# Other joints between the stages of a one-core transformer stack on Trainium2

## The reference

```python
def rms_norm(x, w):
    y = x * lax.rsqrt(jnp.mean(x * x, axis=-1, keepdims=True) + EPS)
    return y * w
# a layer of the first block; the second block has the same shape
mix = mixer(rms_norm(h, norm_pre), ...)            # products, heads, output product
h = h + rms_norm(mix, norm_post)
u = relu(rms_norm(h, mlp_norm_pre) @ w_up)
h = h + rms_norm((u * u) @ w_down, mlp_norm_post)
# second block, last steps
f = (silu(g @ w_gate) * (g @ w_up)) @ w_down       # g = rms_norm(x, ffn_pre_norm)
x = x + rms_norm(f, ffn_post_norm)
x = x + sigmoid(x @ w_ple_gate) * rms_norm(p @ w_ple_proj, ple_norm)
```

## Time and profile before

| what | before |
|---|---|
| median of 3 runs | 1039.75 us (1038.03 to 1039.81) |
| the profiled execution's own time | 1038.76 us |
| its span, first to last instruction | 1037.0 us |
| mean granted TensorE clock | 0.993 |
| PE / PEld / DVE / ACT / POOL busy | 97% / 88% / 71% / 53% / 9% |

### The profile page before, as it was taken

How to read it: one execution, slowest core, us unless ns; L and a number is a source line. 1 busy time by engine, 2 the same in 40 slices (tenths; PEclk the granted TensorE clock), 3 DMA queues, 4 the chain that set the end, 5 groups by cost and what they waited for, 6 DMA issues and landing times.

```text
span 1037.0 us, 18064 instructions
## 1 busy us (share of the span) xinstructions
PE 1002.9 (97%) x6615; PEld 910.1 (88%) x6615; DVE 737.2 (71%) x1095; ACT 550.7 (53%) x824; POOL 89.9 (9%) x94
## 2 busy tenths in 40 slices
PE   6999999999999999998999999998998999999998
PEld 5999988888888989997788888998997888888887
DVE  5787676878764498765977744478778887776466
ACT  5743255655454465655655534445556555555445
POOL 5214101000100200002000100100001000000010
PEclk9999999999999999999999999999999999999999
DMA  8543444466666745434366565625525366665641
GB/s 261 151 124 119 123 122 143 146 198 183 190 185 193 234 132 173 135 122 141 119 208 186 178 193 187 182 74 163 164 82 164 117 183 184 186 196 172 195 145 62
DMA packets 164702, 166.27 MB, mean 160 GB/s; under 512 B 6784, under 2 KB 162832, under 8 KB 164640
## 3 DMA queue, kind: packets, MB, share of 16 engines
q1 hardware_dynamic: 162752, 163.47, 52.3%
q0 software_dynamic: 1056, 1.16, 0.5%
q10 hardware_dynamic: 832, 0.79, 0.3%
HBM read 163.79 MB, written 1.08 MB: 159 GB/s over the span
## 4 chain that ended last, share of the span: by engine, by line
PE 85%; DVE 9%; ACT 3%; issue 2%; DMA 1%; POOL 1%; SPq 0%; DVEq 0%; ACTq 0%; POOLq 0%
PE ps L597 30%; PE ps L596 16%; PE ps L580 4%; PE ps L581 4%; PE ps L582 4%; PE ps L593 3%; PE ps L823 3%; DVE w_lo L1820 2%; PE ps L574 2%; PE ps L576 2%; PE ps L575 2%; PE ps L594 2%; PE ps L587 1%; PE ps L588 1%; PE ps L589 1%
## 5 line engine op out<-in xcount | busy, mean ns | idle before, releaser
L1820 DVE TENSOR_TENSOR w_lo<-w_raw,w_hi 128x1024 fp32r<-128x1024 f32 (+3 forms) x318 | 379.2, 1198 | 156.3 <-ACT w_hi L1302 152.2
L1302 ACT ACTIVATE w_hi<-w_raw 128x1024 fp32r<-128x1024 f32 x302 | 317.4, 1054 | 205.5 <-PE ps L597 91.6
L597 PE MATMUL ps<-xs,w_hi 128*128 128x512 f32 x840 | 296.8, 396 | 0.0
L596 PE MATMUL ps<-xs,w_lo 128*128 128x256 f32 x840 | 235.6, 280 | 0.0
L597 PEld LDWEIGHTS ps<-xs,w_hi 128*128 128x128 f32 x840 | 157.7, 188 | 34.5
L597 PE MATMUL ps<-us,w_hi 128*128 128x512 f32 x498 | 175.2, 393 | 0.0
L596 PEld LDWEIGHTS ps<-xs,w_lo 128*128 128x128 f32 x840 | 158.2, 188 | 5.2 <-DVE xs L1960 1.8
L596 PE MATMUL ps<-us,w_lo 128*128 128x256 f32 x498 | 140.8, 283 | 0.0
L580 PE MATMUL ps<-xs,w_hi 128*128 128x256 f32 x384 | 113.2, 295 | 8.9 <-DVE w_lo L1820 5.4
L597 PEld LDWEIGHTS ps<-us,w_hi 128*128 128x128 f32 x498 | 93.5, 188 | 21.2
L581 PE MATMUL ps<-xs,w_hi 128*128 128x256 f32 x384 | 109.9, 286 | 0.0
(11 more groups left out here) (396 smaller groups left out, 1684.5 us busy)
## 6 DMA issues: line engine op xcount, KB each, us to landing
w_raw<-in_mlp_w_up SPq DMA_DIRECT2D x64, 512.0 KB, 4.3
w_raw<-in_mlp_w_down SPq DMA_DIRECT2D x64, 512.0 KB, 3.5
w_raw<-in_a_w_in SPq DMA_DIRECT2D x32, 512.0 KB, 3.9
w_raw<-in_w_gate SPq DMA_DIRECT2D x22, 512.0 KB, 3.8
w_raw<-in_w_up SPq DMA_DIRECT2D x22, 512.0 KB, 4.5
w_raw<-in_w_down SPq DMA_DIRECT2D x20, 512.0 KB, 4.1
w_raw<-in_w_kv SPq DMA_DIRECT2D x16, 512.0 KB, 4.0
w_raw<-in_w_in SPq DMA_DIRECT2D x16, 512.0 KB, 3.8
```

What stands on the lines that cost most here:

```text
L596: mm(ps[:, bank, 0:S], lo[:, kk, w], x[:, kt, 0:S], start=False, stop=False)
L597: o = mm(ps[:, bank, :], hi[:, kk, w], x[:, kt, :], start=False, stop=last)
L1302: o = fn(dst, raw, ACT.Copy)
L1820: return v.tensor_tensor(d, x, y, ALU.subtract)
```

## The change

It has these parts. "Seam" is used as above.

1. **Roots.** `root`, `root_eps`, `root_heads`, `root_pair` and the attention's root use one activation, `Abs_reciprocal_sqrt`, in place of `Ln` and `Exp`. In the six seams the Newton step's first instruction reads the sum from PSUM and the guess; the separate mean and its EPS go (EPS comes in with the squares, from GpSimd's new constant `eps_sum`, or from `fold`). The table sets are chosen by hand: `abs_reciprocal_sqrt_and_small` in place of `natural_log_exp_and_others`; `exp_and_others` is loaded ahead of each stretch of exponentials (three places), and the root set again behind two of them. The final stage preloads the sigmoid's set in place of the silu's.
2. **Seams.** GpSimd does one addition less there, VectorE does the last two (`take_tail`); ScalarE copies the last tile of `mo`. The first part of unit u+2 of the next product is converted inside the seam (`CONVERTED_IN_SEAM`) instead of behind it.
3. **Banks.** In `up0`, `b_out`, `up1`, `out2` and `gu` the third pair goes to banks 6 and 7 (`pset_of`), and TensorE doesn't wait there for `pair_summed`.
4. **Entry norm.** `f_pre` gets the two foldings on VectorE, and its sum on TensorE falls from 8 tiles to 2. `turn_rstd` of `kv_b`, and the column taken from it, move from quantum 5 to 6. In the second block's mixer the first conversion of `c0` moves ahead of the square of `cq`.
5. **Start.** Five constant matmuls into bank 2 stand before the first unit, behind a wait for the tables' DMA; the quarters' order is (0,0) (0,1) (0,2) (1,0) (1,1) (0,3) (1,2) (1,3), and `setup_rest` comes after all of them.
6. **Heads.** `scale_heads(0)` goes ahead of the conversion of its quantum, the second heads' outputs wait for one scaled tile, not two; `a_out` begins once unit 14 is taken, with quarters in the order (0,0) (0,1) (1,0) ..., and waits for unit 15 only at (1,0); the gating of the third head pair moves behind two `xs` pairs.

The core of the diff (the same edit of `copy_second`/`total` arguments in other loops, and repeated table calls, are left out):

```diff
+OTHER_BANKS = [PAIR0[x] + 2 for x in ("up0", "b_out", "up1", "out2", "gu")]
+def pset_of(p):
+    return 3 if p in OTHER_BANKS else p % 2
+LAST_PAIR = {post: PAIR0[x] + 3 for x, post in DIRECT_LAST.items() if post is not None}
+CONVERTED_IN_SEAM = {u + 2 for u in NEXT_UNIT.values()}
-ENTRY_ADDED = ("x", "kv_b", "mix_pre", "ple")
+ENTRY_ADDED = ("x", "kv_b", "mix_pre", "ple", "f_pre")
...
@@ first_two @@
-                for b, k2 in ((0, 0), (1, 0), (0, 1), (1, 1), (0, 2), (0, 3), (1, 2), (1, 3)):
+                for b, k2 in ((0, 0), (0, 1), (1, 0), (1, 1), (0, 2), (0, 3), (1, 2), (1, 3)):
+                    if (b, k2) == (1, 0):
+                        pe.wait_ge(unit_taken, HGRN_QUANTA // 2)
...
@@ stream @@
-                peel = max(peel, int(two))
+                peel = max(peel, 2 * int(two))
-                        pset = (p0 + b) % 2
-                        wait(pe, pair_summed, pr - 1)
+                        pset = pset_of(pr) if isinstance(i, int) else (p0 + b) % 2
+                        if pset < 2:
+                            wait(pe, pair_summed, pr - 1)
...
@@ sums @@
-                    pe.wait_ge(sq_added, ADD0[name] + 4 + (name in GUARDED))
+                    pe.wait_ge(sq_folded, POSTS.index(name) + 1)
...
@@ start of TensorE @@
             pe.wait_ge(pre_ready, 1)
+            pe.wait_ge(tab_in, 16)
+            keep_streaming(5, bank=2)
-            for b, k2 in ((0, 0), (1, 0), (0, 1), (1, 1), (0, 2), (0, 3), (1, 2), (1, 3)):
+            for b, k2 in ((0, 0), (0, 1), (0, 2), (1, 0), (1, 1), (0, 3), (1, 2), (1, 3)):
-                if (b, k2) == (1, 2):
-                    setup_rest()
...
+            setup_rest()
@@ head_outputs @@
-                wait(pe, oh_scaled, 2 * quad)
+                wait(pe, oh_scaled, quad)
@@ before a_out @@
-            pe.wait_ge(unit_taken, HGRN_QUANTA // 2)
+            pe.wait_ge(unit_taken, HGRN_QUANTA // 2 - 1)
@@ out2 @@
-            pe.wait_ge(pair_summed, p + 1)
...
@@ ScalarE: tail, root, residual @@
                 square_tail(name, unit, pair, 1)
+                fn(mo[:, 7, :], ps[:, 2 * (pair % 2) + 1, 0:S], ACT.Copy).then_inc(pair_summed, 1)
-                fn(guess[:, :], ps[:, NS, 0:S], ACT.Ln, scale=1.0 / NORM_WIDTH.get(name, D),
-                   bias=0.0 if name in GUARDED else eps_col).then_inc(ln_ready, 1)
-                act.wait_ge(ln_ready, ROOT[name] + 1)
-                fn(guess[:, :], guess[:, :], ACT.Exp, scale=-0.5).then_inc(guess_ready, 1)
+                fn(guess[:, :], ps[:, NS, 0:S], ACT.Abs_reciprocal_sqrt, scale=1.0 / NORM_WIDTH.get(name, D),
+                   bias=0.0 if name in POSTS else eps_col).then_inc(guess_ready, 1)
+                    if t == 5:
+                        hi(NEXT_UNIT[name_post] + 2, part=0, in_seam=True)
 root("x")
+            exp_tables()
 root("kv_b")
+            exp_tables()
...
@@ ScalarE: second block @@
-            narrow_high("cq", V_Q, 0)
-            hi(UNIT0["c0"], part=0)
+            narrow_high("cq", V_Q, 0, lambda: hi(UNIT0["c0"], part=0))
@@ ScalarE: last stage @@
-            silu_tables()
+            nc.scalar.preload_act_table_set("sigmoid_and_others")
@@ VectorE: norm @@
-                dve.wait_ge(ln_ready, ROOT[name] + 1)
-                if name in GUARDED:
-                    o = v.tensor_scalar(ms[:, :], ps[:, NS, 0:S], 1.0 / D, None, ALU.mult)
+                dve.wait_ge(guess_ready, ROOT[name] + 1)
+                if name in POSTS:
+                    v.scalar_tensor_tensor(step[:, :], ps[:, NS, 0:S], -0.5 / D, guess[:, :], ALU.mult, ALU.mult)\
+                        .then_inc(ms_ready, 1)
...
@@ VectorE: post @@
+                    if t == 6:
+                        dve.wait_ge(pair_summed, LAST_PAIR[name] + 1)
                     weigh(mo, mo, wcol, t)
...
+                    else:
+                        lo(following + 2, part=0, in_seam=True)
                     low_tile(t)
                     low_tile(t + 1)
@@ VectorE: heads @@
+                if q == 27:
+                    scale_heads(0)
                 lo_q(q + 3)
...
                 if q == 31:
-                    gate_heads(2)
                     low("hgrn", 0, mo, xs)
                     low("hgrn", 1, mo, xs)
+                    gate_heads(2)
@@ VectorE: take_tail @@
-                for t in range(2):
-                    if t == 1:
-                        lo(u + 2, part=0)
-                    dve.wait_ge(sq_ready, READY0[post_name] + 4 + t)
-                    o = v.tensor_copy(mo[:, 6 + t, :], ps[:, 2 * (p % 2) + t, 0:S])
-                o.then_inc(pair_summed, 1)
+                dve.wait_ge(sq_ready, READY0[post_name] + 4)
+                v.tensor_copy(mo[:, 6, :], ps[:, 2 * (p % 2), 0:S])
+                head, tail = 2 * ((SQ0[post_name] + 2) % 4), 2 * ((SQ0[post_name] + 3) % 4)
+                dve.wait_ge(sq_added, ADD0[post_name] + 3)
+                link(v.tensor_tensor(sq[:, head, :], sq[:, head, :], sq[:, head + 1, :], ALU.add))
+                v.tensor_tensor(sq[:, head, :], sq[:, head, :], sq[:, tail, :], ALU.add).then_inc(sq_folded, 1)
+                lo(u + 2, part=0)
@@ VectorE: behind the mix_post seam @@
             post("mix_post", V_MIX_POST, 4, "f", V_F_PRE)
+            fold_squares("f_pre")
+            fold_again()
```

More of the change, by code:

```diff
@@ L737, in sums, with keep_streaming @@
                         sum_pair(name, j)
-            def keep_streaming(n):
+            def keep_streaming(n, bank=B6):
                 for _ in range(n):
-                    mm(ps[:, B6, 0:S], ident, table[:, T_IDENT:T_IDENT + S], start=True, stop=True)
+                    mm(ps[:, bank, 0:S], ident, table[:, T_IDENT:T_IDENT + S], start=True, stop=True)
             pe.wait_ge(ident_in, 16)
@@ L1217, in _ @@
             sums("ple")
-            pe.wait_ge(pair_summed, p + 1)
             for part in range(2):
                 pe.wait_ge(lo_ready, 2 * (u + 2) + part + 1)
-                quantum((2 * (u + 2) + part) % SLOTS, 4 * part, 4, KT - 1, xs_m, "feat", p % 2).then_inc(w_used, 1)
+                quantum((2 * (u + 2) + part) % SLOTS, 4 * part, 4, KT - 1, xs_m, "feat", pset_of(p + 2)).then_inc(w_used, 1)
             pe.wait_ge(pair_summed, p + 2)
@@ L1270, in _, with hi @@
             act.dma_start(table[:, P:T_LEVEL], a["tables"][:, P:T_LEVEL]).then_inc(tab_in, 16)
-            def hi(unit, reg=0, stepu=0, part=0):
+            def hi(unit, reg=0, stepu=0, part=0, in_seam=False):
+                if isinstance(reg, int) and reg == 0 and part == 0 and unit in CONVERTED_IN_SEAM and not in_seam:
+                    return
                 if isinstance(reg, int):
@@ L1303, in hi, with copy_second @@
                 o.then_inc(hi_ready, 1)
-            def copy_second(ready_sem, ready, pset, free, scale=1.0, rows_=P):
+            def copy_second(ready_sem, ready, pset, free, scale=1.0, rows_=P, slot=None):
                 wait(act, ready_sem, ready)
                 wait(act, pair_summed, free)
-                o = fn(tmp[0:rows_, pset, :, :], ps[0:rows_, 2 * pset:2 * pset + 2, S:2 * S], ACT.Copy, scale=scale)
+                o = fn(tmp[0:rows_, pset if slot is None else slot, :, :], ps[0:rows_, 2 * pset:2 * pset + 2, S:2 * S],
+                       ACT.Copy, scale=scale)
                 o.then_inc(pair_copied, 1)
@@ L1534, in _ @@
             residual("a_post", "m0_pre", 0, V_M0_PRE)
-            steps("up0", pairs=16, post=up_post(0), peel=1)
+            steps("up0", pairs=16, post=up_post(0), peel=2)
             def turns():
@@ L1618, in _ @@
             residual("b_post", "m1_pre", 2, V_M1_PRE)
-            steps("up1", pairs=16, post=up_post(16), peel=1)
+            steps("up1", pairs=16, post=up_post(16), peel=2)
             deep_to_mo("down1", 4, "m1_post")
@@ L1637, in narrow_high @@
                 o.then_inc(xs_hi, 1)
+                if then is not None:
+                    then()
                 square(name, 0, ps[:, bank, :].rearrange("p (a t) -> p a t", a=2), None, 0)
@@ L1806, in link, with lo @@
                 dve.wait_ge(dve_chain, chain[0])
-            def lo(unit, reg=0, stepu=0, part=0):
+            def lo(unit, reg=0, stepu=0, part=0, in_seam=False):
+                if isinstance(reg, int) and reg == 0 and part == 0 and unit in CONVERTED_IN_SEAM and not in_seam:
+                    return
                 if isinstance(reg, int):
@@ L1844, in lo, with total @@
                 o.then_inc(lo_ready, 1)
-            def total(pset, dst, rows_=P):
-                return v.tensor_tensor(dst, ps[0:rows_, 2 * pset:2 * pset + 2, 0:S], tmp[0:rows_, pset, :, :], ALU.add)
+            def total(pset, dst, rows_=P, slot=None):
+                return v.tensor_tensor(dst, ps[0:rows_, 2 * pset:2 * pset + 2, 0:S],
+                                       tmp[0:rows_, pset if slot is None else slot, :, :], ALU.add)
             def one(name, j, dst, take=None):
@@ L2601, in gu_body @@
                 for b in range(2):
```

(23 more changed lines are left out.)

83 lines of the change are left out of this document (43 added, 40 removed).

## The result

The changed kernel takes 1021.27 us (median of 4 runs, 1021.0 to 1022.02) against 1039.27 (4 runs): ratio 0.983, 95% interval 0.9813 to 0.9847. The forecast was 1023.2. The profiled execution took 1021.0 us, its span is 1019.2.

What follows compares the result with a forecast made beforehand. The prediction took TensorE, at work 97% of the span, as the bound. Nine terms summed to 16.1 us, giving 1022.7 from the profiled execution and 1023.7 from the median; it forecast 1023.2, range 1016 to 1032.

Steps and rivals of the forecast that it cites:

- Start: First units: new quarter order removes a 2.1 us weight wait and a slow stretch, constants fill a gap; 2.0 us gained.
- Heads: Attention heads: waits of 0.9 for the second scaled tile and 1.2 for the last gate unit go; 1.9 us gained.
- Banks: Third pairs of up0, b_out and up1: 4.2 us of waits for PSUM banks go, b_out stalls 1.3 later; 4.3 us gained.
- Seams: Six seams: 0.55 us each off the root's chain, tile 6 late by 0.5, mix_post gaining 0.1; 1.0 us net.
- kv_b: Product kv_b: delaying by a quantum removes the 0.9 us wait for rstd, less 0.3 at m0_post; 0.6 us gained.
- Second block's entry: Second block's entry: c0's earlier conversion removes a 2.9 us wait and 1.4 of slow clock, VectorE limiting; 2.7 us gained.
- f_pre: Norm f_pre: 16 matmuls become 4, 2.6 us off TensorE, less 0.5 of waiting at the fifth pair; 2.1 us gained.
- Roots: One activation per root: 0.55 us in each seam, and 0.6 us together at the convolution's and attention heads' roots.
- rival A: Whole kernel: stalls come back one step later, VectorE takes TensorE's place, slow stretches move; 9.3 us gained, 1030; chance 21%.
- C: Rival: the root's table set doesn't serve neighbouring copies and squares, two 1.28 us loads per wide root; slower, 1049; chance 4%.
- D: Rival: each seam's nine constant matmuls hold TensorE, bank waits are conversion waits; no gain beyond 2 us, 1039; chance 3%.
- B: Rival: nearly everything arrives, 24 us, 1015; sign: GpSimd's wait in mix_post gone altogether; chance 8%.

Runs made afterwards that it cites:

- u_const: The changed kernel without its five constant matmuls ahead of the first unit, the wait for the tables kept: 1022.97 us, ratio to before 0.9845.
- u_order: The changed kernel with the old order of the first eight quarters and setup_rest ahead of (1,2), constants kept: 1022.96 us, ratio to before 0.9849.
- u_heads: The changed kernel with the whole heads part (point 6 of the change) undone: 1023.39 us, ratio to before 0.9865.
- u_banks: The changed kernel with the third pairs in the two old bank sets and the wait for pair_summed back: 1026.02 us, ratio to before 0.9875.
- u_three: The changed kernel with c0's conversion behind the square, kv_b's turn_rstd at quantum 5 and f_pre's sum over eight tiles again: 1026.20 us, ratio to before 0.9887.
- u_root: The changed kernel with every reciprocal root made of a logarithm and an exponential again, in one table set: 1026.74 us, ratio to before 0.9881.
- x_tables: The changed kernel with two more table loads right ahead of the root in each of the six seams: 1039.23 us, ratio to before 1.0003.

## Why the prediction was right, and where its steps were off

- **Start** (2.0, came 1.9). The size was right, partly by luck, the reason half so. The step had the constants "at no cost" and without a gain, and let the slow stretch go because the hole at 15 us closed. In its profile u_const is 1.4 to 1.6 late at a slow stretch of its own, u_order as much. Two new waits on `w_lo` came between 31 and 40 us (0.6 and 1.1); a third, 0.4, stood in the kernel before as well.
- **Heads** (1.9, came 2.3). Both waits went and `xs` wasn't late; u_heads gives 2.0.
- **Banks** (4.3, came 4.8; 4.9 in u_banks). The predicted stall ahead of `b_out`'s last pair is there, 1.4 against 1.3.
- **Seams** (1.0, came 1.2). Tile 6 late by 0.4 in five of them, where the step had 0.5, nothing in `m1_post`, as worked out. In `mix_post` the step failed: the two weighings were to shrink from 2.37 us to 0.9 "with GpSimd silent", but GpSimd's one remaining addition stands beside the first, so only the second shrank (0.94 to 0.47) and the two take 1.89. They also start 0.6 later against TensorE's work than before. The step's sum was off besides: 803.7 less 1.5, plus 0.4 and 0.9, is 803.5, not 804.3. The sum of squares came 0.6 later, not 0.1 earlier, and the slow stretch that was missing in this profile paid for it: that the term comes out is luck.
- **`kv_b`** (0.6, came 1.2). Mis-sized, and put down to the wrong edit: u_three shows the delay worth nothing beside the others; what took the wait away is argued above, not shown.
- **Second block's entry** (2.7, came 3.1) and **`f_pre`** (2.1, came 1.9). The step "VectorE can come forward by at most 3.1" held: TensorE gains 4.6 at 690 us and gives back 1.5 by 709. The fifth pair waits 0.6 for 0.5.
- **Roots.** The two terms, 3.3 in the seams and 0.6 elsewhere, stand against 2.7 and 2.5 in u_root. The second was too small by 1.9. Only the sum with the edits that eat it (conversion ahead of tile 6, one more table load at the start) came out right, and that is luck too.
- **Last stage** (0.9, came 0.7). No run undoes it by itself, nor VectorE's last two additions (`take_tail`).
- **The clock.** "From four to one or two": none in the first profile, one of double length in the second. The four in the profile of before were one draw, so the 1.4 for each that the banks, the entry and rival A are worked out with isn't fixed either. The 1.7 us between the sum (16.1) and the span (17.8) is `kv_b` 0.6, banks 0.5, heads 0.4, entry 0.4 and seams 0.2, less 0.5 at the start, `f_pre` and the last stage, each rounded.

Rival A had part of the mechanism (some of the stall comes back: 1.4 of 4 in `b_out`, 1.3 of 4.3 in the entry) but not the size; C's price was confirmed by x_tables, D is refuted by it. B's sign, GpSimd's wait gone, is there by name only: VectorE's of 2.7 us stands in its place.

## What to carry to other kernels

Where TensorE is at work 97% of the span, add up its waits and slow stretches, then take each one only down to the next engine's own line: here that gave the gain of every place within 0.6 us, though not always for the right reason. An edit's worth in its place depends on the others: undone alone, the parts here add up to more than the whole, and the delay in `kv_b` to nothing. What stands ahead of a chain's last piece on the engine that makes it (a conversion ahead of tile 6, a weighing ahead of a sum) delays it, by 0.4 and up to 2.3 us here. Moved behind it or into a slack stage it cost nothing that shows in four seams and in `down2`; in `kv_b` it cost 0.9. And look at the granted clock of every execution before a slow stretch of one profile is entered as a gain.
